# Turning the last expert product: gated prompt tokens stationary, value rows 512 wide into eight PSUM banks, sampled tokens' rows gathered

## The reference, cut to what matters

```python
idx = i1 * N_KEYS + i2
gate = jax.nn.softmax(cs, axis=-1)
a = jnp.einsum('cd,chkd->chk', xc, peer_u[idx])
act = (jax.nn.gelu(a.astype(jnp.float32), approximate=False) * gate).astype(xc.dtype)
return jnp.einsum('chk,chkd->cd', act, peer_v[idx])
...
return _layer_norm(ALPHA * h + _peer(h, w_query, sub_keys, peer_u, peer_v), ln2_g, ln2_b)
```

## Time and profile before

| what | us |
|---|---|
| median of 3 runs | 2291.38 (2290.71 to 2291.55) |
| span of the profiled execution | 2289.8 |
| median less the span | 1.6 |
| PE busy | 2268.3 |
| DVE busy | 1491.2 |
| POOL busy | 1442.5 |
| ACT busy | 884.7 |

### The profile page before, as it was taken

How to read it: one execution, slowest core, us unless ns; L and a number is a source line. 1 busy time by engine, 2 the same in 40 slices (tenths; PEclk the granted TensorE clock), 3 DMA queues, 4 the chain that set the end, 5 groups by cost and what they waited for, 6 DMA issues and landing times.

```text
span 2289.8 us, 48588 instructions
## 1 busy us (share of the span) xinstructions
PE 2268.3 (99%) x17591; PEld 2259.5 (99%) x17591; DVE 1491.2 (65%) x2713; ACT 884.7 (39%) x1109; POOL 1442.5 (63%) x750
## 2 busy tenths in 40 slices
PE   9999999999999999999999999999999999999997
PEld 9999999999999999999999999999999999999997
DVE  3984564354659986556556561478777778777755
ACT  5444453345544444333333333333333333333334
POOL 4876667776677777767767667755555555554025
PEclk9999999999999999999999999999999999999998
DMA  7554446554455555666666666887767777777653
GB/s 255 171 197 152 143 137 206 208 182 156 148 165 187 190 182 191 202 213 215 214 213 217 214 213 217 273 277 237 259 233 246 253 251 258 242 247 242 214 171 110
DMA packets 150512, 475.26 MB, mean 208 GB/s; under 512 B 19568, under 2 KB 42352, under 8 KB 149872
## 3 DMA queue, kind: packets, MB, share of 16 engines
q1 hardware_dynamic: 116944, 416.43, 55.5%
q10 hardware_dynamic: 24264, 40.93, 4.9%
q0 software_dynamic: 9216, 16.81, 2.4%
HBM read 433.21 MB, written 43.28 MB: 208 GB/s over the span
## 4 chain that ended last, share of the span: by engine, by line
PE 93%; DVE 5%; DMA 1%; issue 1%; ACT 1%; SPq 0%; DVEq 0%; ACTq 0%
PE ps L1562 29%; PE ps L1556 29%; PE ps L1557 29%; PE ps L1845 1%; DVE F L1092 1%; DVE F L1093 1%; PE ps L1598 1%; PE ps L1771 1%; DMA F<-gelu_scratch,F 1%; PE ps L1790 0%; DVE b_lo L1106 0%; PE ps L1605 0%; DVE R L1121 0%; PE ps L646 0%; ACT R L1046 0%
## 5 line engine op out<-in xcount | busy, mean ns | idle before, releaser
L759 POOL TENSOR_TENSOR w_lo<-raw,w_hi 128x1024 fp32r<-128x1024 f32 x452 | 1095.1, 2446 | 542.6 <-ACT w_hi L816 511.8
L816 ACT ACTIVATE w_hi<-raw 128x1024 fp32r<-128x1024 f32 x690 | 693.8, 1053 | 653.5 <-PE ps L1562 576.7
L1556 PE MATMUL ps<-a_hi,w_hi 128*128 128x288 f32 x3072 | 826.0, 295 | 0.0
L1557 PE MATMUL ps<-a_lo,w_hi 128*128 128x288 f32 x3072 | 824.3, 295 | 0.0
L1556 PE MATMUL ps<-b_hi,w_hi 128*128 128x288 f32 (+2 forms) x2432 | 629.2, 290 | 0.4 <-ACT w_hi L816 0.4
L1557 PE MATMUL ps<-b_lo,w_hi 128*128 128x288 f32 (+2 forms) x2432 | 626.7, 289 | 0.0
L1556 PEld LDWEIGHTS ps<-a_hi,w_hi 128*128 128x128 f32 x3072 | 577.1, 188 | 2.4 <-issue 2.2
L1557 PEld LDWEIGHTS ps<-a_lo,w_hi 128*128 128x128 f32 x3072 | 578.4, 188 | 0.1
L1562 PE MATMUL ps<-a_hi,w_lo 128*128 128x288 f32 x3072 | 468.5, 294 | 0.0
L791 POOL DMA_INDIRECT sample_rows<-in_peer_v,F x256 | 301.0, 1176 | 262.2 <-PE ps L1562 208.0
L1556 PEld LDWEIGHTS ps<-b_hi,w_hi 128*128 128x128 f32 x2432 | 457.9, 188 | 0.9 <-issue 0.8
(11 more groups left out here) (259 smaller groups left out, 1440.9 us busy)
## 6 DMA issues: line engine op xcount, KB each, us to landing
raw<-in_peer_u SPq DMA_DIRECT2D x256, 512.0 KB
raw<-in_peer_v SPq DMA_DIRECT2D x256, 512.0 KB
raw<-in_w_in SPq DMA_DIRECT2D x96, 512.0 KB
gelu_scratch<-F ACTq DMA_DIRECT2D x32, 576.0 KB, 6.0
gate_scratch<-g_stage ACTq DMA_DIRECT2D x36, 512.0 KB, 6.0
F<-gelu_scratch SPq DMA_DIRECT2D x32, 576.0 KB
raw<-in_w_out SPq DMA_DIRECT2D x32, 512.0 KB
raw<-in_w_query SPq DMA_DIRECT2D x32, 512.0 KB
```

What stands on the lines that cost most here:

```text
L759: pool.tensor_tensor(wl[:, j, s], raw[:, j, s], wh[:, j, s].bitcast(F32), ALU.subtract).then_inc(lo_ready, 1)
L816: act.activation(wh[:, k, s], raw[:, k, s], ACT.Copy).then_inc(hi_ready, 1)
L1556: pe.matmul(out, w, mh(k), start=(n == 0), stop=False)
L1557: pe.matmul(out, w, ml(k), start=False, stop=False)
```

## The change

The last product is turned. The gated prompt tokens become stationary (128 experts by 128 tokens, two tiles), and the value rows move, 512 output columns wide, that is one unit pair, a "super": 64 supers of 48 matmuls of 512 columns. The sums stay in all eight PSUM banks (4 column banks for each of 2 token tiles) through the whole stage, so there are no evictions; they begin with h, put in by 64 identity matmuls. ALPHA goes into the gates in place of a multiplication of R. w_hi and w_lo have a second pair of buffers, in R's place. The sampled tokens' part is gathered for all output columns: 16 row gathers a slot and one for gelus, with no paced waits. Adds stand at supers 0, 1, 2, 4, 6 and so on to 60. The gates have 64 steps in place of 72 (WITH = 8). The last eight units of peer_u are lowered by DVE. The last norm is computed token-major with bn_stats, and y is turned by transposes at the end.

```diff
-BEFORE, WITH = 5, 9
-TOKS = T // (WITH * 8)
+BEFORE, WITH = 5, 8
+TOKS = SEQ // (WITH * 8)
...
+TOK_TILES = 2
+COL_BANKS = 4
+SUPERS = BLOCKS * COL_BANKS
+LOW_DVE = 8
 SLOTS = PH * TOPK // 4
+ROWS = 16
 RING = 2
-V_LAST = 120
+def added_at(k):
+    return k if k < RING else int(1.98 * (k - 1) + 0.6)
+ADD_AT = {added_at(k): k for k in range(SLOTS)}
...
-            ve.tensor_scalar(R[:, :, :], R[:, :, :], ALPHA, None, ALU.mult).then_inc(y_init, 1)
...
# GpSimd
-            for k in range(SLOTS):
+            def gather_rows(k):
                 n = k % RING
-                if k >= RING:
-                    pool.wait_ge(slot_used, k - RING + 2)
                 for r in range(ROWS):
-                    paced(k, r)
                     pool.indirect_dma_start(VROWS[:, n, r * P:r * P + P], None, v_rows,
                                             bass.IndirectOffsetOnAxis(ap=VIDX[:, k, r:r + 1], axis=0))\
-                        .then_inc(row_in[n][r], 16)
+                        .then_inc(row_in[n], 16)
...
+            pool.wait_ge(rows_named, 1)
+            for k in range(RING):
+                gather_rows(k)
+            for m in range(2):
+                pool.wait_ge(a_stored[m], 16 * BLOCKS + 1)
+            for k in range(RING):
+                gather_gelu(k)
+            for k in range(RING, SLOTS):
+                pool.wait_ge(slot_used, k - RING + 2)
+                gather_rows(k)
+                gather_gelu(k)
...
# ScalarE
+            def hi_v(u):
+                n, k = u // 2, u % 2
+                if n == 1:
+                    act.wait_ge(h_added, 1)
+                else:
+                    act.wait_ge(outs_done, OUT0["peer_v"] + max(n - 1, 0) + 1)
...
# VectorE
+            for n in range(SUPERS - 1):
+                b, q = divmod(n, COL_BANKS)
+                lower_super(n + 1)
+                if b + 1 < BLOCKS:
+                    if q == 0:
+                        ve.wait_ge(blk_in[(b + 1) % 2], 64 * ((b + 1) // 2 + 1))
+                        ve.wait_ge(outs_done, OUT0["peer_v"] + n + 1)
+                    for e in (2 * q, 2 * q + 1):
+                        gate((b + 1) % 2, e)
+                if n in ADD_AT:
+                    add_slot(ADD_AT[n])
+                if b == BLOCKS - 1 and q > 0:
+                    ve.wait_ge(outs_done, OUT0["peer_v"] + n + 1)
+                    for t in range(TOK_TILES):
+                        row_stats(ve, P, 1 + t, q - 1, y_bank(t, q - 1))
...
+            other = VROWS[:, 0, :]
+            ve.wait_ge(slot_used, SLOTS + 1)
+            link(ve.tensor_copy(other[0:64], ACC[64:128]))
+            link(ve.tensor_tensor(ACC[0:64], ACC[0:64], other[0:64], ALU.add))
+            link(ve.tensor_copy(other[0:NS], ACC[NS:2 * NS]))
+            link(ve.tensor_tensor(ACC[0:NS], ACC[0:NS], other[0:NS], ALU.add))
...
# TensorE
+            def v_high(n, s, e, t):
+                pe.matmul(y_sum(n, t), tokens(bh, s, e, t), rows(WH, n, e), start=False, stop=False)
+                pe.matmul(y_sum(n, t), tokens(bl, s, e, t), rows(WH, n, e), start=False, stop=False)
+            def v_low(n, s, e, t, stop=False):
+                return pe.matmul(y_sum(n, t), tokens(bh, s, e, t), rows(WL, n, e), start=False, stop=stop)
...
+            pe.wait_ge(z_sample, 1)
+            pe.wait_ge(bank0_free, 1)
+            for e in range(KT):
+                last = pe.transpose(y_bank(0, 0)[:, e * NS:e * NS + NS], VROWS[0:NS, 0, e * P:e * P + P], ident[0:NS, 0:NS])
+            last.then_inc(ys_turned, 1)
+            for e in range(8):
+                v_high(last_super, 1, e, 1)
```

More of the change, by code:

```diff
@@ L614, in norm_sums @@
             pe.matmul(LNP[1], ones[:, :], SQ[:, (KT - 1) % 2], start=False, stop=True).then_inc(ln_pe, 1)
[L616 to L638, removed]
         def values(pe, c, probs):
@@ new lines, in hi_v @@
+            def hi_v(u):
[4 more added lines that the diff above has]
+                    act.wait_ge(outs_done, OUT0["peer_v"] + max(n - 1, 0) + 1)
+                for h in range(2):
+                    act.wait_ge(loaded[2 * k + h], 16 * ((UNIT0["peer_v"] - FIRST_UNITS) // 2 + n + 1))
+                    s = slice(h * HU, h * HU + HU)
+                    act.activation(WH[n % 2][:, k, s], raw[:, k, s], ACT.Copy).then_inc(hi_ready, 1)
@@ new lines, in _, with y_act_bank @@
+            for u in range(1, 2 * SUPERS):
+                hi_v(u)
+            row_sqrt(act, NS, 0)
+            def y_act_bank(t, c):
+                act.wait_ge(y_turned, COL_BANKS * t + c + 1)
+                for q in range(4):
+                    e = 4 * c + q
+                    last = act.activation(YT[:, e, P * t:P * t + P], y_bank(t, c)[:, P * q:P * q + P], ACT.Identity,
+                                          scale=V("g2")[:, e:e + 1], bias=V("b2")[:, e:e + 1])
+                last.then_inc(y_act, 1)
@@ L1460, in gate, with lower @@
+                ve.tensor_tensor(bl[:, 8 * s + e, 0:SEQ], AB[:, s, e, 0:SEQ], bh[:, 8 * s + e, 0:SEQ].bitcast(F32),
                                  ALU.subtract).then_inc(act_ready, 1)
-            def take(o, j, i):
-                n = v_cols(j // 2)
-                ve.wait_ge(outs_done, OUT0["peer_v"] + i + o + 2)
-                ve.tensor_tensor(R[:, j, 0:n], R[:, j, 0:n], ps[:, ROT[(o + 2) % 4], 0:n], ALU.add).then_inc(ev_dve, 1)
-            def lower(u, j):
+            def lower(unit, high, low, j):
@@ new lines, in _, with y_dve_bank @@
+            row_variance(ve, link, NS, 0)
+            ve.wait_ge(outs_done, OUT0["peer_v"] + SUPERS)
+            for t in range(TOK_TILES):
+                row_stats(ve, P, 1 + t, 2, y_bank(t, 2))
+            mean, r = row_rstd(ve, link, NS, 0)
+            ve.tensor_scalar(other[0:NS], ACC[0:NS], mean, r, ALU.subtract, ALU.mult).then_inc(z_sample, 1)
+            def y_dve_bank(t, c):
+                ve.wait_ge(y_turned, COL_BANKS * t + c + 1)
+                for q in range(4):
+                    e = 4 * c + q
+                    last = ve.tensor_scalar(YT[:, e, P * t:P * t + P], y_bank(t, c)[:, P * q:P * q + P],
+                                            V("g2")[:, e:e + 1], V("b2")[:, e:e + 1], ALU.mult, ALU.add)
+                last.then_inc(y_dve, 1)
@@ L1539, in _, with product @@
         @block.tensor
         def _(pe):
-            def product(bank, slot, tiles, mh, ml, u, m_wait=None, cols=T, low=None, ends=True):
+            def product(bank, slot, tiles, mh, ml, u, m_wait=None, cols=T, low=None):
                 out = ps[:, bank, 0:cols]
@@ L1813, in _, with u_unit @@
             pe.wait_ge(n_lo, KT // 2)
-            def u_unit(i, j, back=0):
-                unit("peer_u", ev_act, ACT_EV0["peer_u"] - back, i, j, a_op(ah), a_op(al))
+            def u_unit(i, j, back=0, low=None):
+                unit("peer_u", ev_act, ACT_EV0["peer_u"] - back, i, j, a_op(ah), a_op(al), low=low)
             for j in range(8):
@@ new lines, in _ @@
+            pe.wait_ge(act_ready, 8)
+            pe.wait_ge(ident_set, 1)
+            for t in (1, 0):
+                if t == 0:
+                    pe.wait_ge(ev_act, ACT_EV0["peer_u"] + 128)
+                for e in range(KT):
+                    for h in (ah, al):
+                        last = pe.matmul(y_bank(t, e // 4)[:, e % 4 * P:e % 4 * P + P], h[:, e, t * P:t * P + P],
+                                         ident_r[:, :], start=(e % 4 == 0 and h is ah), stop=False)
+            last.then_inc(h_added, 1)
@@ new lines, in _ @@
+            with pe.Fori(0, BLOCKS // 2 - 1) as i:
+                for k in range(8):
+                    v_super(i, k)
+            for k in range(7):
+                v_super(BLOCKS // 2 - 1, k, ends=(k >= COL_BANKS))
+            last_super = SUPERS - 1
+            high_in(2 * last_super + 1)
+            for e in range(8):
+                v_high(last_super, 1, e, 0)
+            low_in(2 * last_super + 1)
+            for e in range(8):
+                last = v_low(last_super, 1, e, 0, stop=(e == 7))
@@ L1900, in _axes @@
+            for c in range(COL_BANKS):
+                turn(0, c)
+            for e in range(8):
+                last = v_low(last_super, 1, e, 1, stop=(e == 7))
+            last.then_inc(y_summed, 1)
+            for c in range(COL_BANKS):
+                turn(1, c)
 def _axes(a, shape, order):
```

392 lines of the change are left out of this document (172 added, 220 removed).

## The result

The changed kernel takes 2364.96 us (median of 4 runs, 2362.73 to 2371.29), the kernel before 2291.47 in the same comparison (2290.71 to 2291.74): a ratio of 1.0325, 95% interval 1.0311 to 1.0340. It is slower by 73.5 us. The forecast was 2395 in a range of 2300 to 2435: direction, cause and range held, and the loss was put 30 us too high. The profiled execution is the slowest of the four: 2371.29 us, its span 2369.5.

A forecast was written before the change was run, and what follows sets the result against it. POOL's 17 indirect DMAs a slot, lengthened by DVE, were taken as the bound: add 0 ends near 1507, thirty slots of 27.8 us reach 2341, the rest ends at 2393, forecast 2395 us, range 2300 to 2435 (0.8).

The forecast's parts named there:

- The slot's price: POOL's time for one slot's 17 indirect DMAs, in two supers: 27.8 us, thirty slots 834 us.
- the undisturbed 21.3: A slot's 17 indirect DMAs on POOL at 1.25 us from start to start, without delay by DVE: 21.3 us.
- The contiguous run of lowerings: Four DVE lowerings back to back, 4.6 us, pass two gathers instead of 3.7: 2.0 us lost, 4.0 for two runs.
- The add: DVE's add over 2048 columns, once a slot: one gather waits up to 2.5 us, on average 1.9.
- The upper bound of 29.0: Highest price of a slot on POOL, if each gate costs a gather half a microsecond: 29.0 us.
- The start: Start of the peer_v stage: peer_u ends at 1488.8, identity matmuls take 6.4 us, super 0 starts at 1495.2.
- The matmul: A 512-column matmul on PE takes 226 ns, its extra over the columns staying fixed; a super takes 10.86 us.
- the line through the two widths: Alternative estimate for a 512-column matmul, extrapolated from the rows at 256 and 288 columns: 232 ns.
- the rival where PE bounds: POOL keeps up with its gathers and PE sets the time: 2214 us, chance 0.16.
- The delay's way to PE: DVE idles some 10 us before each add; PE waits for w_lo and w_hi some 6 us per two supers.
- DMA as the bound: Rival: DMA engines sustain only 254 GB/s, a super takes 12.5 us, total 2317 us; chance 0.06.
- Gathers disturbed only as today: Rival: DVE lengthens gathers on POOL no more than before, 25.1 us a slot, total 2314 us; chance 0.10.

The follow-up runs named there:

- e1: The changed kernel with peer_v laid out so that eight gathers of 1 KB rows replace sixteen of 512 B a slot: 2232.38 us.
- e2: The changed kernel with four gathers of 2 KB rows a slot in place of sixteen of 512 B: 2232.61 us.
- e4: The changed kernel with each DVE lowering of 1024 columns issued as two of 512, same gathers and bytes: 2280.77 us.
- e5: The changed kernel with 14 of the 16 row gathers a slot issued from the third slot on: 2298.8 us.
- e6: The changed kernel with 12 of the 16 row gathers a slot issued from the third slot on: 2235.26 us.
- e7: e2 with the matmuls of one token tile (one PSUM bank) ordered before those of the other: 2230.64 us.

## Why the prediction was right, point by point

- **What bounds.** Right: 17 indirect DMAs a slot on POOL, lengthened by DVE. e1 and e2 (fewer DMAs, same bytes) and e4 (shorter DVE operations, same DMAs) each remove the loss from their own side, and e5 and e6 give the slope.
- **The slot's price, the term that was mis-sized.** Forecast 27.8 us, measured 26.8; over 30 slots 30 us. That this equals the error of the total is a coincidence: the start was 2.5 us later and the tail 5 longer than forecast, and the median lies 6 below the profiled execution. In the slot shown (26.9) the undisturbed 21.3 held. The contiguous run of lowerings cost 2.04 (two gathers of 1.97 for 0.95), as forecast. The second run, taken as contiguous too and priced at 2.0, cost 1.8 (gathers of 1.61, 1.63, 1.05 and 1.27): DVE waits inside it for ACT's rounding, which waits for raw's loads, and gathers pass in the gaps. The add cost 1.4 where I had 1.9. Two short waits for gates (1.15 each) make 0.4, forecast 0.5. The means of all 30 slots are the same (3.8, 1.4 and 0.4), so half of the error is the add. The upper bound of 29.0 is 29.2 by its own terms.
- **The start.** Super 0 begins at 1496.95, forecast 1495.2. The identity matmuls took 7.1 us and not 6.4, and peer_u ended 1.1 later than forecast, at 1489.9. The third slot's first gather starts at 1509.45; I had 1507 for the add that frees its place.
- **The matmul.** 226 ns forecast, 232.6 measured; the line through the two widths, 232, was the better choice. Here it hid behind POOL. In the rival where PE bounds it would have been 62 x 0.30 = 19 us: that rival's sum, 2214, becomes 2233, and e1 and e2 measured 2232.4 and 2232.6. It is the sum closest to its run, though of a kernel that the change was not, and partly by luck: in e2 super 0 starts 1.5 us later than in that sum, and super 62 to the end takes 1.4 less.
- **Two figures of the Trainium skill.** The Trainium skill, TensorE: Matmul & The Clock Gate, "Back-to-back issue gap", gives 215.8 ns at 512 columns for a matmul by itself, and 131 for a stream of them; the trace has 232.6 and agrees with neither. The Trainium skill, SBUF — State Buffer, "SBUF: two separate sides", has a DMA released some 115 ns after DVE ends. The rows after show 0.82 us again, but that is the end of the gather's instruction; when it was released they do not show, so the two figures need not be of the same thing. The prediction's step from 115 ns to a gather at every lowering's end, and so to no loss, fails either way.
- **The delay's way to PE.** Right in kind: DVE waits for the slot, and PE for DVE. But PE meets it once in four supers, for about 7 us, at the gated tokens (b_lo) and not at w_lo and w_hi every second super. DVE's wait ahead of an add is 6.6 us on the mean, forecast 10. The granted clock fell too (0.93 over the stage); whether DVE's idle time absorbed that, as forecast, was only argued from POOL having no idle time, and no run kept the clock up beside the same gathers.
- **The end.** The last gather ends at 2313.8 (forecast 2341), the last add at 2317.8 (2346). From there to z_sample's arrival, 2345.5, it is 27.7 us (forecast 27), and from there to the end 24.0 (forecast 20). The tail was forecast 5 us too short, which offsets part of the slot's 30.
- **The rivals.** DMA as the bound fell to e1 (280 GB/s at a share of 0.79, with PE never idle). Gathers disturbed only as today would have been 25.1 a slot; the measured 26.8 lies between that and the forecast.

## What to carry to other kernels

Count the instructions that a busy engine's neighbour has to issue and price one from start to start, gap included: here 17 requests of 1.25 us, and not their bytes, decided against a change that saves 59 us once they are fewer. A gather costs POOL about the same for rows of 512 B, 1 KB or 2 KB, so lay the table out for long rows before shortening anything else. Where one engine's operations hold another's requests, their length relative to the other's period can matter more than their sum: in e4 the lowerings took longer in sum (eight at 0.63 for four at 1.13), and halving them was worth 84 us, where two requests less a slot (e5) were worth 66.

## What the runs showed of the hardware that was not expected

- **What a matmul takes beyond its columns grows with the width.** Against the columns alone at 2.4 GHz it is 12.5 ns at 256, 13.3 at 288 and 19.3 at 512 (232.6 less 213.3). The 128-column identity matmuls come 111 ns apart (7.09 us for 64), 58 above their 53. Changes of bank are not the cause (e7); the cause is open.
- **The gap of 0.30 us between indirect DMAs stays** when no wait on a semaphore stands between them, so it belongs to the request and not to the wait: it is 0.30 or 0.31 before each of the 509 that follow the first of the stage.
- **The length of a row does not change what a gather costs POOL.** One group for each, over all the gathers of row pieces (ns min/median/max, first and last start, forms). The kernel after, rows of 512 B:
```profile
L746 POOL DMA_INDIRECT sample_rows<-in_peer_v,F x512: 940/1048/2946, 1433.1 to 2311.6; - x171
```
e1, rows of 1 KB:
```profile
L746 POOL DMA_INDIRECT sample_rows<-in_peer_v,F x256: 941/949/2812, 1432.4 to 2141.1; - x128
```
e2, rows of 2 KB:
```profile
L746 POOL DMA_INDIRECT sample_rows<-in_peer_v,F x128: 941/1162/1997, 1432.9 to 2135.2; - x128
```
The shortest is 940 or 941 ns in all three; only the meetings with DVE differ.
- **After 7.05 us of idleness PE ran some 11 matmuls at the granted clock's lower level** (0.50, 0.42 to 0.43 us from start to start) before it was back at 1.00: about 2 us for this wait, and 1.4 to 2.9 over the 15. In e2 3.8 us of idleness cost 1.5.
